# GpSimd's third weight sums of the down projections asked for ahead of the next first sum, and a later first role in two-pair sets

## The reference

```python
def swiglu(x, w_gate, w_up, w_down):
    return (jax.nn.silu(x @ w_gate) * (x @ w_up)) @ w_down
...
x = x + 0.5 * swiglu(rms_norm(x, g_norm[l, 0]), w_ffn_gate[l, 0], w_ffn_up[l, 0], w_ffn_down[l, 0])
h = rms_norm(x, g_norm[l, 1])
...
x = x + 0.5 * swiglu(rms_norm(x, g_norm[l, 2]), w_ffn_gate[l, 1], w_ffn_up[l, 1], w_ffn_down[l, 1])
```

## Time and profile before

| what | value |
|---|---|
| median of 3 runs | 2457.02 us (2455.48 to 2464.59) |
| profiled execution, its own time | 2457.78 us |
| its span, first to last instruction | 2455.7 us |
| TensorE busy (PE) | 2402.1 us, 98% |
| VectorE busy (DVE) | 1858.7 us, 76% |
| ScalarE busy (ACT) | 1336.1 us, 54% |
| GpSimd busy (POOL) | 544.4 us, 22% |
| granted TensorE clock, mean | 0.995 of full |
| down-weight sums by GpSimd: first, third | 60 and 60 |

### The profile page before, as it was taken

How to read it: one execution, slowest core, us unless ns; L and a number is a source line. 1 busy time by engine, 2 the same in 40 slices (tenths; PEclk the granted TensorE clock), 3 DMA queues, 4 the chain that set the end, 5 groups by cost and what they waited for, 6 DMA issues and landing times. The chain is left out here.

```text
span 2455.7 us, 48881 instructions
## 1 busy us (share of the span) xinstructions
PE 2402.1 (98%) x18377; PEld 2261.9 (92%) x18377; DVE 1858.7 (76%) x3709; ACT 1336.1 (54%) x2873; POOL 544.4 (22%) x422
## 2 busy tenths in 40 slices
PE   9899999999999999999999999999999999999998
PEld 9899999888778999999988999999996699999998
DVE  7887979422787888787925889787928878887865
ACT  6555656201785655555622655555618856555554
POOL 1222222354000121222135222222131002222210
PEclk9999999999999999999999999999999999999999
DMA  5557575333863465756523775766467544766642
GB/s 146 121 116 144 106 148 101 95 116 97 304 237 94 97 140 103 144 115 140 104 79 127 187 143 115 139 127 126 107 227 265 209 112 94 145 125 126 139 101 82
DMA packets 423237, 334.20 MB, mean 136 GB/s; under 512 B 20641, under 2 KB 383834, under 8 KB 423010
## 3 DMA queue, kind: packets, MB, share of 16 engines
q1 hardware_dynamic: 281296, 246.98, 32.2%
q0 software_dynamic: 133136, 65.82, 21.9%
q10 hardware_dynamic: 8578, 18.37, 2.1%
HBM read 314.98 MB, written 16.13 MB: 135 GB/s over the span
## 5 line engine op out<-in xcount | busy, mean ns | idle before, releaser
L997 PE MATMUL PS<-x_area,w_area 128*128 128x320 f32 x3096 | 483.1, 310 | 2.3 <-ACT PS L1804 2.3
L997 PEld LDWEIGHTS PS<-x_area,w_area 128*128 128x128 f32 x3096 | 461.6, 188 | 2.7 <-ACT PS L1804 2.6
L1718 ACT ACTIVATE w_area<-R 128x512 fp32r<-128x512 f32 (+2 forms) x583 | 325.5, 567 | 204.9 <-DVE R L2414 92.3
L2393 DVE TENSOR_TENSOR w_area<-R,w_area 128x512 fp32r<-128x512 f32 (+2 forms) x583 | 357.7, 615 | 87.1 <-ACT w_area L1718 86.5
L2393 DVE TENSOR_TENSOR r_area<-R,r_area 128x512 fp32r<-128x512 f32 (+2 forms) x437 | 265.8, 617 | 94.4 <-ACT r_area L1718 88.8
L1804 ACT ACTIVATE PS<-PS 128x320 f32<-128x320 f32 x438 | 178.3, 416 | 215.6 <-PE PS L997 189.9
L997 PE MATMUL PS<-r_area,w_area 128*128 128x320 f32 x1584 | 266.4, 311 | 10.7 <-ACT PS L1804 6.2
L1718 ACT ACTIVATE r_area<-R 128x512 fp32r<-128x512 f32 (+2 forms) x437 | 247.7, 567 | 47.2 <-DVE R L2414 20.2
L997 PEld LDWEIGHTS PS<-r_area,w_area 128*128 128x128 f32 x1584 | 239.1, 188 | 18.3 <-ACT PS L1804 11.2
L1226 PE MATMUL PS<-w_area,xn_hi 128*128 128x512 f32 x800 | 251.5, 396 | 0.5 <-DVE xT L2578 0.3
L997 PE MATMUL PS<-r_area 128*128 128x320 f32 x1392 | 236.5, 311 | 2.2 <-DVE r_area L2648 1.8
(11 more groups left out here) (348 smaller groups left out, 4152.6 us busy)
## 6 DMA issues: line engine op xcount, KB each, us to landing
R<-in_w_ffn_up_dram SPq DMA_DIRECT2D x45, 512.0 KB, 5.2
R<-in_w_ffn_gate_dram SPq DMA_DIRECT2D x43, 512.0 KB, 5.1
R<-in_w_ffn_up_dram SPq DMA_DIRECT2D x86, 256.0 KB, 4.1
R<-in_w_ffn_up_dram POOLq DMA_DIRECT2D x86, 256.0 KB, 4.8
R<-in_w_ffn_gate_dram SPq DMA_DIRECT2D x82, 256.0 KB, 4.6
R<-in_w_ffn_gate_dram POOLq DMA_DIRECT2D x81, 256.0 KB, 5.5
R<-in_w_ffn_down_dram SPq DMA_DIRECT2D x52, 384.0 KB, 3.9
R<-in_w_ffn_down_dram SPq DMA_DIRECT2D x88, 192.0 KB, 3.7
```

Source lines behind the costliest of these rows:

```text
L997: last = pe.matmul(PS[:, bank, 0:HT], a[:, k, :], b, start=(start and opens), stop=(k == n - 1 and a is lo), skip_group_check=True)
L1718: act.activation(role_parts(f, g, s, role)[0], role_source(f, g, s, role), ACT.Copy).then_inc(sem("early_cast") if key in EARLY_COUNT else ...
L2393: dve.tensor_tensor(lo, role_source(f, g, s, role), hi.bitcast(F32), ALU.subtract).then_inc(sem("early_split") if key in EARLY_COUNT else ...
```

## The change

Two things change. In `add_sums`, in all 60 down sets, the third sum of set n+1 is put ahead of the first sum of set n+2 instead of behind it. And `first_late` is now true for d2, d3 and d4 of a two-pair group: W11 of the following set is split behind S4 and S3 of the present one.

```diff
 def first_late(at):
-    return False
+    return is_down(*at) and not opens_down(*at) and GROUPS[at[0]] == 2
...
                 order = chain(f)
                 for at in order[:2]:
                     first_sum(at)
+                ahead = [at for at in order[1:] if is_down(*at)]
                 for n, at in enumerate(order):
-                    third_sum(at)
+                    if at not in ahead:
+                        third_sum(at)
+                    if n + 1 < len(order) and order[n + 1] in ahead:
+                        third_sum(order[n + 1])
                     if n + 2 < len(order):
                         first_sum(order[n + 2])
```

## The result

| | before | after |
|---|---|---|
| median of 4 runs | 2457.51 us (2455.48 to 2464.59) | 2529.28 us (2526.02 to 2530.48) |
| span of the profiled execution | 2455.7 us | 2528.2 us |
| granted TensorE clock, mean | 0.995 | 0.985 |

The change makes the kernel slower: the ratio of times is 1.0285, with an interval of 1.0262 to 1.0308, some 72 us. The prediction had the direction and the mechanism, but a quarter of the size, and its range ended at 2490.

The account below looks back on a forecast made before the run. TensorE, busy 2402.1 of 2455.7 us, was taken as the bound; losses of 6 us in two-pair and 12 us in three-pair groups, given as 18.5, made 2474.2, or 2475.5 against the median, range 2456 to 2490.

Parts of the forecast that it names:

- The new chain of waits: Down sets: S2 sum, third sum, next first sum, its landing, then next S2 sum and S3, beginning anew each set.
- Landing in three-pair groups: First sum of d3 lands after 5.2 us, 1.06 us late; eleven groups lose 12 us, bounds nothing to 27.
- rival D: First sums land 6.6 us and more behind another sum, losing 27 + 15 us, or 2499; chance 0.07.
- Landing in two-pair groups: First sum of d3 lands after 4.2 us, 0.9 late; period 6.8 us, 7.9 for d4; four groups lose 6 us.
- Busy times stay: Whole kernel: no instruction is added or removed, so the engines' busy times stay the same.
- That S3 comes later by what the landing is late: Three-pair groups, S3 of d2: fixed distance from S2 sum to S3, so TensorE stands still 1.06 us more.
- The sum: Two-pair and three-pair losses, 6 + 12, given as 18.5 us on a span of 2455.7, making 2474.2.
- The rule from the Trainium skill: First sums in down sets: by this rule they land ahead of both slots and the 18 us would be none.
- Rival C: First sums land in time everywhere and gaps in down sets go: 8 us gained, 2449; chance 0.10.
- A: The forecast: first sums are late by about a microsecond in each group, 2468 to 2488; chance 0.53.
- B: First sums in down sets are late by half or less, 6 us lost, so 2463; chance 0.30.
- What would show it: VectorE idle ahead of d3's and d4's S2 sums, three-pair gap about 1.3 us, landings of 5 us behind third sums.

Follow-up runs that it names:

- s3_first: The changed kernel with VectorE's next S2 sum behind S3's and W11's low parts, and ScalarE's copy ahead of S1's high part; 2473.9 us, ratio 1.0063.
- s3_vector_only: The changed kernel with VectorE's next S2 sum behind S3's and W11's low parts, ScalarE's copy left behind S1's high part; 2512.86 us, ratio 1.0216.

## Where the prediction was right, and where it was wrong

- *What bounds the kernel.* Right. All that changed is TensorE's idle time and its own busy time; no other engine became a bound.
- *The new chain of waits* (S2 sum, third sum, first sum, landing, next S2 sum, with S3 behind the sum on VectorE and the copy behind S1's high part on ScalarE). Right, and shown: the timelines have it step for step, and `s3_first` and `s3_vector_only` free exactly what was said to be queued and get 55 and 16 us back.
- *Landing in three-pair groups, 5.2 us, 1.06 us late, 12 us.* The mis-sized term. The first sum in the group that was worked out lands after 6.4 us; as it goes out 0.77 us and not 1.27 us behind the start of the third one, that is 7.2 us from the third sum's issue instead of 6.5. It made a gap of 2.10 us, and the average of the eleven groups is 2.6, so 25 us. In the eleven groups it lands 6.3 to 7.9 us after its issue. I took the value from the earlier trace rows because its SP loads had this size; the groups came out nearer to the 6.6 us and more of the earlier trace rows, which I had as the end of the range and as rival D. The trace of before had held more: the third sums of d3 in its eleven three-pair groups, ten of them directly behind a first one and one 0.34 us later, land after 4.9 to 7.3 us, with a median of 6.2, so that the 5.3 of rows 16 was the second lowest. With 6.2 the same working gives 2.1 us a group and 23 in all.
- *Landing in two-pair groups, 4.2 us, and a period of 6.8, 6 us.* The other mis-sized term. The first sums of d3 and d4 land 5.2 to 6.8 us after their issue, the two periods are 7.6 to 9.2 and 10.0 to 10.8 us, and the loss is 22 us. The row for a sum directly behind another one had said 5.0 to 6.3, and the middle towards the undisturbed 3.3 was chosen against it. The largest part is the last step, with n1's first sum: it had the 5.0 us of a sum with none just ahead of it and took 7.5 to 8.4, and the gaps ahead of S3 of d4 (4.61, 4.61, 4.33 and 2.39 us) are half of the 31.7. TensorE needs 6.4 us a set, and this chain starts anew from each set's own S2 sum, so every period above that costs again.
- *Busy times stay.* The step that failed outright, 22 us. It was written for instruction counts and is true of them, but TensorE's clock was put at no cost. The three gaps of the earlier trace rows were about a microsecond and none brought a slow stretch; 16 of the 21 gaps of 1.4 to 4.6 us were followed by 3 to 7 us at half clock. The prediction had taken the gaps' lengths and not what comes behind them.
- *That S3 comes later by what the landing is late* (three-pair groups). Right: a gap of 2.10 us, against 1.88 us of VectorE's idle time and the 0.24 that was there.
- *The sum.* Its terms, 1.0 + 1.5 + 2.1 + 1.6 and eleven times 1.06, make 17.9 us and not 18.5; it changes nothing in the rest.
- *The rule from the Trainium skill, "DMA: Bandwidth & Descriptors", section on the anatomy of one DMA on the GpSimd path* (2.0 us plus bytes by 436 KB per us). By it my estimate was 2.3 us for 128 KB and 2.45 for 192. The trace doesn't agree: the down sums directly behind another one took 4.8 to 8.4 us. Rival C, which it gave, is out, and so are A and B in size. D is the nearest: its mechanism held and its 2499 still was 30 us short, 22 of them the clock.
- *What would show it.* The waits stood at the named places: VectorE idle ahead of S2 sums, the gap at S3 of d2 (2.0 us and more instead of "about 1.3"), the third sum of d4 behind W11's split, landings of about 5 us and more.

## What to carry to other kernels

Before a DMA is moved behind another one on its queue, find the instruction that waits for it and list what its in-order engine holds behind that wait: here one sum and one copy that were moved gave back 55 of 72 us, with the DMAs still in the bad order. Price a DMA that goes out directly behind another by rows in which one does, and let the undisturbed row be the bound, not half of the average, above all where the landing feeds a chain that starts anew each step. And price a new TensorE gap by its own length plus the slow stretch that may follow: here 47 us more of gaps came with 22 us more of busy time.

## What was unexpected of the hardware

- Gaps of 2 to 4.6 us brought stretches of 3 to 7 us at about half the clock, and with them 22 us of TensorE's busy time. It isn't the length of the gap alone: that of 2.74 us ahead of 2141.55 did not bring one, that of 2.10 us did (the group at 2256.21 took 1.83 us). What decides it isn't settled here.
- A first sum that is queued on GpSimd directly behind a third one starts 0.71 us after it and not after its 1.19 us, and is itself 1.71 us long. The two issues together take 2.4 us, as two separate ones did.
- Two sums that land after 3.3 us alone don't land after 4.2 us together. The medians of the page's part on DMA issues say so for all down sums (first and third), the last number being us from issue to landing, of after:

```profile
R<-in_w_ffn_down_dram POOLq DMA_DIRECT2D x88, 192.0 KB, 5.9
...
R<-in_w_ffn_down_dram POOLq DMA_DIRECT2D x32, 128.0 KB, 4.4
```

Before they were 4.5 and 3.6 us.
